# A 25th place for expert weights, requests without a limit, and the last norm's rows by transposes

## The reference

```python
e_idx, gate = route(xf, w_router, b_router)      # best group of 4, its top 2 of 32
y = moe_ffn(xf, e_idx, gate, w_gate, w_up, w_down)
#   per expert: h = silu(xb @ w_gate[e]) * (xb @ w_up[e]);  h @ w_down[e]
x = layer_norm(DEEPNORM_ALPHA * x + y, ln_g[2], ln_b[2])
```

## Time and profile before

| | us |
|---|---|
| three runs | 1108.01, 1110.08, 1111.56; median 1110.08 |
| the profiled execution | 1108.52 |
| its span | 1106.8 |
| PE busy | 1033.0 (93%) |
| DVE, ACT, POOL busy | 343.2, 251.5, 101.6 |

### The profile page before, as it was taken

One profiled execution on the slowest core, in us unless ns is written; L12 is line 12 of the kernel. 1 busy time (PEld: TensorE's weight loads), 2 busy tenths in 40 slices (PEclk: granted clock), 3 DMA queues, 4 the chain that ended last, 5 costly groups with the idle time before them and its releaser, 6 DMA issues.

```text
span 1106.8 us, 15722 instructions
## 1 busy us (share of the span) xinstructions
PE 1033.0 (93%) x6596; PEld 516.4 (47%) x6596; DVE 343.2 (31%) x724; ACT 251.5 (23%) x510; POOL 101.6 (9%) x141
## 2 busy tenths in 40 slices
PE   8999999999898999999999999999999999887896
PEld 4444455557655554566544733333333333333342
DVE  0179623234655645203215511111111111011015
ACT  2341122234435520013401111111111111011023
POOL 2000100000000000100000211111111111110123
PEclk9999999999999999999999999999999999999999
DMA  8012320211222150553833899999999999999995
GB/s 274 23 65 76 115 77 2 78 43 51 63 77 80 76 191 1 181 236 113 311 121 121 341 417 419 423 419 418 419 416 422 415 423 414 416 417 408 417 415 210
DMA packets 57462, 265.73 MB, mean 240 GB/s; under 512 B 7122, under 2 KB 8274, under 8 KB 32560
## 3 DMA queue, kind: packets, MB, share of 16 engines
q1 hardware_dynamic: 51200, 255.49, 58.2%
q0 software_dynamic: 4960, 8.15, 2.0%
q10 hardware_dynamic: 1232, 1.08, 0.3%
HBM read 256.56 MB, written 16.25 MB: 246 GB/s over the span
## 4 chain that ended last, share of the span: by engine, by line
PE 34%; DMA 20%; DVE 3%; ACT 1%; issue 1%; DVEq 0%; SPq 0%; ACTq 0%
PE cpair L2051 7%; DMA ring<-in_w_exp_up 7%; PE bank L2061 6%; DMA xT<-in_w_exp_up 4%; DMA ring<-in_w_exp_down 4%; PE tpair L2051 4%; DMA keys<-in_w_exp_up 3%; DMA ar<-in_w_exp_down 3%; PE bank L1890 2%; PE bank L1870 2%; PE tpair L1890 1%; PE bank L1863 1%; PE cpair L1890 1%; PE tpair L1870 1%; PE cpair L1870 1%; PE bank L2033 1%
## 5 line engine op out<-in xcount | busy, mean ns | idle before, releaser
L2051 PE MATMUL cpair<-ring,xgT 128*64 128x512 f32 x344 | 115.0, 598 | 6.4 <-DMA xT<-in_w_exp_up 4.1
L2491 DVE TENSOR_TENSOR hs<-cpair,hs 64x512 f32<-64x512 f32 x21 | 14.5, 693 | 252.4 <-ACT hs L2273 252.4
L2273 ACT ACTIVATE hs<-cpair 64x512 f32<-64x512 f32 x21 | 12.4, 588 | 235.5 <-PE cpair L2051 235.5
L2051 PEld LDWEIGHTS cpair<-ring,xgT 128*64 128x64 f32 x344 | 36.0, 138 | 58.4 <-issue 58.4
L1793 POOL DMA_INDIRECT y_rows<-ye,tabs x30 | 30.5, 1018 | 352.2 <-ACT xgt L2279 331.3
L922 PE MATMUL bank<-xT,ring 128*128 128x512 f32 x128 | 60.9, 606 | 0.0
L2051 PE MATMUL tpair<-ring,xgT 128*64 128x512 f32 x168 | 56.5, 593 | 0.0
L365 PE MATMUL bank<-xT,ring 128*128 128x512 f32 x112 | 48.5, 593 | 0.0
L2491 DVE TENSOR_TENSOR hs<-tpair,hs 64x512 f32<-64x512 f32 x11 | 7.6, 693 | 125.5 <-ACT hs L2273 125.5
L941 PE MATMUL tpair<-ring,mixT 128*128 128x512 f32 x96 | 42.0, 594 | 0.0
L2061 PE MATMUL bank<-ring,hT 128*64 128x512 f32 x128 | 32.4, 653 | 4.1 <-DVE hT L2495 4.1
(11 more groups left out here) (479 smaller groups left out, 1913.5 us busy)
## 6 DMA issues: line engine op xcount, KB each, us to landing
ring<-in_w_exp_up SPq DMA_DIRECT2D x32, 1024.0 KB, 10.2
ring<-in_w_exp_gate SPq DMA_DIRECT2D x32, 1024.0 KB, 10.4
ring<-in_w_exp_down SPq DMA_DIRECT2D x16, 1024.0 KB, 10.6
ring<-in_w_in SPq DMA_DIRECT2D x6, 2048.0 KB, 8.1
ring<-in_w_mem_kv SPq DMA_DIRECT2D x4, 2048.0 KB, 10.3
opening<-in_w_exp_gate SPq DMA_DIRECT2D x8, 1024.0 KB, 10.3
mixT<-in_w_exp_down SPq DMA_DIRECT2D x8, 1024.0 KB, 10.5
mixT<-in_w_exp_gate SPq DMA_DIRECT2D x8, 1024.0 KB, 10.4
```

What stands on the lines that cost most here:

```text
L2051: last = nc.tensor.matmul(bank[b][m * CAP:(m + 1) * CAP, :], xgT[:, j, h, :], w(m, h)[:, j * DE:(j + 1) * DE], start=(k == 0), stop=(k == ...
L2491: V.tensor_tensor(hb, bank[1 + e % 3][CAP:P, :], sil, ALU.mult).then_inc(h_done, 1)
```

## The change

- `lists_at` is now the 25th place, and `extra` is two tiles. SP asks pieces 21, 22 and 23 right behind piece 20 (22 after `lg_full`, 23 after `lt_full`), piece 24 at `tabs_done`; it waits for neither `asked` nor `comb_done`. From piece 25 on a request waits only for its place.
- The space: `xgt` shrinks to `xg`, the gathered rows alone. Half of `x2T` gets a tile of its own for the routing (`x2_high`), `first_rows` writes into `ye` and DVE adds in place, `combT` and `comb` move to freed places. `first_rows(e)` now waits for the scatter of expert e - 2 out of the same buffer; DVE does `out_rows(e - 1)` before `hidden(e)`.
- `comb` is built in expert 28 from the comparisons made anew (`last_hit`), and turned in expert 29. Before, DVE built it between the routing's tables.
- `ln3`: in expert 28 PE transposes a broadcast column of `cols` for each of the 16 blocks of 128, and ACT copies the banks. POOL's `spread`, `ones3` and PE's L2135 go.
- At the end `down(31)` comes before `combined(0, 0)`.

```diff
-        NPL = len(places) + 2
+        NPL = len(places) + 3
...
-        extra = sb("extra", [P, HALF])
-        places += [extra[:, :], lists_at[:, :]]
+        extra = [sb(f"extra{i}", [P, HALF]) for i in range(2)]
+        places += [extra[0][:, :], extra[1][:, :], lists_at[:, :]]
...
                     load_piece(sp, 20)
+                    load_piece(sp, 21)
+                    sp.wait_ge(lg_full, 2)
+                    load_piece(sp, 22)
+                    sp.wait_ge(lt_full, 2)
+                    load_piece(sp, 23)
 
                 def experts():
-                    sp.wait_ge(asked, 1)
-                    load_piece(sp, NPL - 3)
                     sp.wait_ge(tabs_done, 1)
-                    load_piece(sp, NPL - 2)
-                    sp.wait_ge(comb_done, 1)
                     load_piece(sp, NPL - 1)
                     for n in range(NPL, len(stream)):
                         e, i, h = stream[n - NPL]
                         sp.wait_ge(w_read, read_at[e, DN if i == 2 else GU, h])
-                        piece_here(sp, n - 4)
                         load_piece(sp, n)
...
-                        if e == LAST - 2:
-                            down_read(pool, e)
-                            pool.memset(ones3, 1.0).then_inc(spread_done, 1)
-                            for h, name in enumerate(("n3_g", "n3_b")):
-                                at = ROWS[name][0]
-                                pool.tensor_tensor(spread[:, h, :, :], ident[:, :].unsqueeze(1).to_broadcast([P, KT, P]),
-                                                   cols[:, at:at + KT].unsqueeze(2).to_broadcast([P, KT, P]), ALU.mult)\
-                                    .then_inc(spread_done, 1)
...
-                        if e == 0:
+                        if e == LAST - 2:
                             tables_turned()
...
+                    def last_norm(h):
+                        pe.wait_ge(ln3_here, 2 * h)
+                        at = ROWS[("n3_g", "n3_b")[h]][0]
+                        for hf in range(2):
+                            for j in range(4):
+                                c = at + 4 * hf + j
+                                last = nc.tensor.transpose(bank[6 + hf][:, j * P:(j + 1) * P],
+                                                           cols[:, c:c + 1].to_broadcast([P, P]), ident[:, :])
+                            last.then_inc(ln3_full, 1)
 
                     tokens(0)
                     for e in range(NE):
-                        if e == LAST:
-                            last_norm()
                         products_of(e)
+                        if e == LAST - 3:
+                            last_norm(0)
...
+                    down(f)
                     pe.wait_ge(y_scaled, LAST)
-                    pe.wait_ge(ln3_here, 4)
+                    pe.wait_ge(comb_read, 2)
                     combined(0, 0, True)
-                    down(f)
                     combined(1, 0, True)
...
                         if e >= 2:
-                            act.wait_ge(y_scaled, e - 1)
-                        nc.scalar.activation(xrow[:, e % 2, :], xg[:, e % 2, :], ACT.Copy,
+                            act.wait_ge(y_out[e % 2], 16 * (e // 2))
+                        nc.scalar.activation(ye[:, e % 2, :], xg[:, e % 2, :], ACT.Copy,
                                              scale=tabs[:, e, 3:4].bitcast(F32)).then_inc(x_done, 1)
...
+                    def combination():
+                        gu_read(dve, LAST - 3)
+                        for k in range(TOP_K):
+                            rows = slice(k * NT, (k + 1) * NT)
+                            V.tensor_tensor(last_hit[:, rows, :], ls.caps[:, :].unsqueeze(1).to_broadcast([P, NT, 2 * CAP]),
+                                            ls.place[:, rows].unsqueeze(2).to_broadcast([P, NT, 2 * CAP]), ALU.is_equal)\
+                                .then_inc(last_hits, 1)
...
                     for e in range(NE):
+                        if 0 < e < LAST:
+                            out_rows(e - 1)
                         hidden(e)
-                        if e:
+                        if e == LAST:
                             out_rows(e - 1)
...
                         turned(e)
+                        if e == LAST - 3:
+                            combination()
```

More of the change, by code:

```diff
@@ L1406, in hybrid_decoder_trunk @@
         xg_here = [sem(f"xg_here{s}") for s in range(2)]
-        xgt = sb("xgt", [P, 2, D])
-        xg, xrow = (xgt[:, i, :].rearrange("p (b c) -> p b c", b=2) for i in range(2))
+        xg = sb("xg", [P, 2, D // 2])
         def slots_of(dve, ls):
@@ L1593, in hybrid_decoder_trunk @@
             <= read_at[LAST - 2, DN, 1]
-        yb = [free[t].rearrange("p (k d) -> p k d", k=TOP_K) for t in range(NT)]
-        hs2 = free[4][:, 0:DE]
-        hb2, sil2 = hs2[0:CAP, :], hs2[CAP:P, :]
[L1597 to L1607, removed]
+        ln3 = free[0].rearrange("p (h d) -> p h d", h=2)
+        last_hit = free[1][:, 0:D].rearrange("p (r c) -> p r c", c=2 * CAP)
+        comb = free[1][:, D:2 * D].rearrange("p (a t c) -> p a t c", a=2, t=NT)
+        combT = free[2][:, 0:2 * S].rearrange("p (a s) -> p a s", a=2)
+        yb = [free[3 + t].rearrange("p (k d) -> p k d", k=TOP_K) for t in range(NT)]
+        ob = [free[(7, 10)[t // 2]][:, (t % 2) * D:(t % 2 + 1) * D] for t in range(NT)]
+        spare = free[11].rearrange("p (b d) -> p b d", b=2)
+        x3 = [yb[t][:, 0, :] for t in range(NT)]
+        further_piece = lambda i, h: free[(5, 6, 7, 10, 11, 12)[2 * i + h]]
+        hs2, yf, xf = (free[8][:, i * 512:(i + 1) * 512] for i in range(3))
+        hb2, sil2 = hs2[0:CAP, :], hs2[CAP:P, :]
+        tabs2 = free[8][:, 1536:1536 + 4 * NE].bitcast(I32).rearrange("p (e f) -> p e f", f=4)
+        ls2 = Lists(kept, free[9])
+        ln3_full, ln3_here, last_hits = sem("ln3_full"), sem("ln3_here"), sem("last_hits")
         acc = ((6, 7), (3, 1), (2, 4), (5, 0))
@@ L1840, in body @@
                             pool.wait_ge(f_ys, g)
-                            scatter(rowc[:, :], ye[:, 0, :]).then_inc(f_out, 16)
+                            scatter(rowc[:, :], yf).then_inc(f_out, 16)
                             pool.wait_ge(f_out, g * 16)
@@ L2125, in body @@
                             down_terms(5, hT[:, 0, :, :], further_piece, 1).then_inc(f_y, 1)
[L2127 to L2135, removed]
-                                                 spread[:, h, 4 * hf:4 * hf + 4, :].rearrange("p j q -> p (j q)"),
-                                                 start=True, stop=True).then_inc(ln3_full, 1)
+                    def last_norm(h):
[7 more added lines that the diff above has]
+                            last.then_inc(ln3_full, 1)
                     tokens(0)
                     for e in range(NE):
-                        if e == LAST:
-                            last_norm()
                         products_of(e)
+                        if e == LAST - 3:
+                            last_norm(0)
                         if e == LAST - 1:
@@ L2315, in experts @@
                             first_rows(e + 1)
+                        if e == LAST - 3:
+                            last_norm(1)
                     act.wait_ge(set_done, 1)
@@ L2470, in routing @@
                     link(dve, V.tensor_copy(more_i[:, :], ls.most_f[:, :]))
-                    def combination(a):
-                        for t in range(NT):
-                            link(dve, V.tensor_scalar(comb[:, a, t, :], ls.hit[:, t, :], last_oh[:, 0, t, a:a + 1], None,
-                                                      ALU.mult))
-                            last = V.scalar_tensor_tensor(comb[:, a, t, :], ls.hit[:, NT + t, :],
-                                                          last_oh[:, 1, t, a:a + 1], comb[:, a, t, :], ALU.mult, ALU.add)
-                        return last
                     link(dve, V.tensor_copy(last_oh[:, :, :, :], oh[:, 0:TOP_K, :, LAST - 1:NE]))
@@ L2499, in out_rows @@
                         dve.wait_ge(x_done, e + 1)
-                        if e >= 2:
-                            dve.wait_ge(y_out[e % 2], 16 * (e // 2))
-                        if e == 0:
-                            dve.wait_ge(comb_full, 1)
                         down_read(dve, e)
-                        V.scalar_tensor_tensor(ye[:, e % 2, :], bank[5 if e < LAST else 0][:, :], tabs[:, e, 2:3].bitcast(F32), xrow[:, e % 2, :],
+                        V.scalar_tensor_tensor(ye[:, e % 2, :], bank[5 if e < LAST else 0][:, :], tabs[:, e, 2:3].bitcast(F32), ye[:, e % 2, :],
                                                ALU.mult, ALU.add).then_inc(y_scaled, 1)
+                    def combination():
[5 more added lines that the diff above has]
+                                .then_inc(last_hits, 1)
+                        dve.wait_ge(last_hits, TOP_K)
+                        for a in range(2):
```

(6 more changed lines are left out.)

44 lines of the change are left out of this document (20 added, 24 removed).

## The result

The changed kernel takes 1114.87 us (median of 6 runs, 1112.83 to 1117.4), the kernel before 1109.59 beside it (6 runs, 1107.83 to 1111.56): ratio 1.0050, 95% interval 1.0036 to 1.0063. It is slower by 5.3 us, beyond what the prediction called measurable and above its range.

A forecast was written before the change was run, and what follows sets the result against it. The DMA engines' fixed amount to move after 617 us was taken to bound the kernel, PE's floor 11.4 us away. Terms -0.55 + 0 + 0 + 0.3 = -0.25 us gained, added to 1110.08, gave 1110.3; range 1104.5 to 1113.5.

The forecast's parts named there:

- What bounds the kernel: From 640 us the DMA engines are never idle; their fixed amount sets the end, PE's own floor 11.4 us away.
- D: How much later PE starts expert 0's tokens because the first gather lands behind queued pieces: 3.8 us.
- the 25th place's worth is nearly all given back: At the first reuse of a place: of 2.5 us, a gain of 4.1 - 3.8 = 0.3 us stays.
- the sum: All parts of the change over the whole kernel: -0.55 + 0 + 0 + 0.3 = -0.25 us gained.
- a low clock at 632 costs 1.7 us before the first place is read: PE after its 3.6 us wait for the first gather: 1.7 us lost, even chance, middle -0.55 with the gather's part.
- POOL's third add is tied to the reads: At the end PE arrives 2.2 us earlier, but the add follows the y_rows landings: 0.3 us gained.
- No limit of four, 0 us: SP's piece requests in steady state: engines already busy 1.01, no idle time to win, taken as 0.
- rival 2: The DMA rate rises with the deep queue by 1% or more: 4.4 us on top, 1105.9; chance 0.16.
- Scatter order, moved tables: Scatter landings of 6.3 to 7.0 us stay hidden under 18 us; moved work at experts 28 and 29 costs 0.
- 1 (lead kept): First gather lands in time, D near 0: gain 4.0 us, 1106.1; chance 0.10.
- 3 (small transfers wait for the depth): Every expert's small transfers wait for the queue's depth, holding first_rows on ACT: 195 us, about 1305; chance 0.04.
- 4: First gather served strictly after the pieces asked before it: D = 5.8, gain -3.1 us, 1113.2; chance 0.08.

The follow-up runs named there:

- r4_dummies: Changed kernel with 31 more pairs of dummy transposes on PE before expert 0's tokens (UNREAD[3] 34 instead of 3); 1115.86 us, ratio 1.0049.
- r9_cover: Changed kernel with 15 more pairs of dummy transposes before expert 0's token transposes, to fill PE's wait for the first gather; 1111.08 us, ratio 1.0012.
- r7_both: r1_asked with piece 21 asked right behind piece 20 and PE's last products for all tables ahead of those with POOL's rows; 1106.25 us, ratio 0.9969.
- r1_asked: Changed kernel with SP again waiting for the first gather to be asked before piece 21; 1110.57 us, ratio 1.0006.
- r3_both: Changed kernel with both the wait for the first gather's request before piece 21 and the limit of four back; 1111.04 us, ratio 1.0001.
- r10_after_again: Changed kernel without any edit, measured again in a second session; 1114.46 us, ratio 1.0033.
- r2_limit: Changed kernel with the limit of four back (SP waits for piece n - 4 before asking for n); 1113.48 us, ratio 1.0028.
- r8_before_nolimit: Kernel before the change with only the limit of four taken out; 1110.55 us, ratio 1.0005.
- r12_before_early21: Kernel before the change, with 24 places, and piece 21 asked right behind piece 20; 1111.37 us, ratio 1.0007.
- r5_tail: r1_asked with PE's last products for all tables ahead of all products with POOL's rows; 1108.96 us, ratio 0.9990.
- r11_both_limit: r7_both with the limit of four requests put back; 1107.61 us, ratio 0.9978.

## Why the prediction was wrong

It forecast 1110.3 and no measurable change; the kernel is slower by 5.3 us. By its own steps:

- **What bounds the kernel.** Held. The DMA share is 1.01 from 645 on in both. Counted from the request of piece 20, and less the engines' idle time from 623 to 645 (1.0 to 7.2 us), POOL's first add comes at 461.9 to 463.9 us in all fourteen profiles. So it follows the idle time within 2 us; the latest of them, r4_dummies and the two with both edits, are 1.9 us behind the changed kernel, and why is open.
- **D and "the 25th place's worth is nearly all given back".** Held: D was forecast 3.8 us; the tokens were turned at 633.53 against 628.22 + 1.57 for the shift, 3.74. r9_cover, where nothing else of the loss before 645 is left, is idle 3.7 us as before; the sum gave 0.3 us less.
- **"By the rows a low clock at 632 costs 1.7 us before the first place is read; I give it an even chance."** This is the first step that failed, in size and in its chance; that a low clock would cost time was right. It was there in all three profiles with the wait of 3.6 us left uncovered, it cost 2.8 us (9.90, 9.94 and 9.98 us for 32 products, 7.11 with the wait covered), and the engines' idle time grew by 3.1 us, where the sum had a loss of 0.55. The 1.7 came from the only rows at hand: 5.35 us against 3.65 for sixteen products. It is not a fixed price: sixteen products took 6.42 us in the changed kernel at 1072.44. Neither the number of products nor the wait just ahead sorts these sizes: 2.97 us came before a loss of 1.7 in rows 9, 3.59 before 2.8 here, 1.31 before 2.8 at 1070, and 0.52 before 1.7 in r7_both at 640. What sets them stays open; the mistake was to take one case as the price. The granted clock in the window at 634, right after the wait, is 0.53, a mean over the two levels. The Trainium skill's rule (TensorE: Matmul & The Clock Gate, "What's actually happening"), that the low clock is the default and activity releases it, agrees with that window.
- **"POOL's third add is tied to the reads. PE can only take what stood between 1091.14 and 1091.78; I count 0.3 us of it."** The second step that failed, in sign. PE does arrive early, and gains nothing by it. The third add is not tied to the reads alone: with VectorE's norm beside it it takes 3.1 us where the sum had 2.36, so the slack it counted was not there. Of the eight profiles with the tail as the change leaves it six show PE waiting 3.0 to 3.2 us for the third add, and four of these (r1_asked, r3_both, r9_cover, r10_after_again) run on at low clock: from the first pair of products with POOL's rows to the third 6.7 to 6.8 us, against 3.8 in the two others and in the kernel before. That is 3.0 us for those executions. In the other two, the changed kernel's first profile and r2_limit, a low clock in expert 31's products makes PE late instead, and the tail is 24.8 and 24.9 us. Over the eight its mean is 25.2 us; it is 22.8 to 22.9 in the kernel before, r8_before_nolimit and r12_before_early21. r5_tail, which splits the wait, has a tail of 22.7 us and gains 1.8 us over r1_asked by the ratios.
- **No limit of four, 0 us.** Held in the time: r8_before_nolimit stands at 1.0005, and r2_limit and r3_both are not told apart from the same kernels without the limit. Not in the trace: the mean rate from 645 to 1076 rose to 421 GB/s from 418, 0.7%, which would be 3.1 us, two thirds of rival 2. It was given back at the end, where the queue drains unevenly (below): in r7_both and r11_both_limit POOL's first add, less the shift by piece 20's request, comes at 1082.0 and 1082.1, without and with the limit.
- **Scatter order, moved tables.** Held: the scatters land in 6.6 us, ACT's 2.0 us of waiting for them in three experts reach nobody, and PE waits nowhere for the moved work.
- **The rivals.** 1 (lead kept) fell; 3 (small transfers wait for the depth) fell clearly, with a request landing 27 us after it was made while scatters took 6.6, and 6.8 with four at most in the queue. The Trainium skill's rule that engines take turns between queues (DMA: Bandwidth & Descriptors, "Queues, rings and completion order") agrees with these scatters. 4 named the right direction and nearly the size for the wrong reason: D was 3.74, not 5.8.

The sum with the measured terms is 4.1 - 3.74 - 2.8 = -2.4 us for the DMA engines, and 22.9 - 25.2 = -2.3 for the tail, together -4.7; measured -5.3 and, the second time, -4.3 by the medians. How often an execution has the low clock in the tail is known only from these few profiles, so that term is the softest. For a single profile the split above is firm; for the median it is an estimate.

## What to carry to other kernels

Before filling a gap in a busy queue, look at what small transfer was quick because of the gap, and let as many requests pass ahead of it as the engines can finish before it comes: one here, not three. A wait of some 3 us on PE is priced with the slow products that may follow it: 1.7 to 3 us in most of these traces, nothing in some. Work taken off PE ahead of such a wait only lengthens it, so the work left should be laid into the wait or between two. Where places and order depend on each other, test both alone and together: each alone left the engines idle for 3.4 us, the two together for 1.1, and that is some 2 us of r7_both's 3.4; the rest is the tail's.

## What the runs showed of the hardware that was not expected

- *A low clock need not cost time.* In r7_both sixteen down products of expert 0 took 5.35 us instead of 3.65 at 640.18 (granted clock 0.66 over 640 to 645), with no wait over 0.75 us among expert 0's products, and it is the fastest kernel. PE waits 11 us for pieces after that, so the 1.7 us are likely taken out of those waits; no run takes the slow products alone away.
- *Without the limit the transfers fade out instead of stopping.* The windows of the changed kernel, and then of r2_limit, which asks for piece 20 only 0.2 us earlier and has the limit, show it in the DMA share of the same two stretches. Over the next 4 us it is 0.13 and 0.17, over the 8 us ahead 0.98 and 1.01. That the 16 engines get ahead of one another in a deep queue would explain it; no run measured an engine by itself.

```profile
1084.00:1088.00 4.00, 3.48 (x19) 1.50 (x15) 1.17 (x2) 0.44 (x2) 0.50 (x1) 1.00 0.78 317
1088.00:1092.00 4.00, 4.00 (x20) 1.41 (x18) 0.75 (x1) 0.00 (x0) 3.82 (x2) 1.00 0.46 186
```

```profile
1084.00:1088.00 4.00, 3.48 (x19) 1.58 (x17) 1.18 (x2) 0.68 (x2) 0.00 (x0) 1.00 1.02 411
1088.00:1092.00 4.00, 4.00 (x22) 1.29 (x20) 0.75 (x1) 0.00 (x0) 3.78 (x2) 1.00 0.88 354
```

- *POOL and VectorE slow each other at the end.* POOL's adds of 128x1024 take 2.35 us alone and 3.1 to 3.3 (6.42 for two in r7_both) beside VectorE's norm. A VectorE pass that takes 1.28 us behind POOL's last add took 3.13 in the changed kernel beside it, while that add kept its 2.35.
- *A shift that has nothing to do with the change.* From 457 us of the span on, 32 products took 12.06 us in the changed kernel's profile and 10.59 before; the time of piece 20's request, 616.6 to 620.4 over all profiles, varies from one profile to the next, with and without the change (617.2, 618.7 and 619.9 in the three kernels with 24 places). A span is compared from an event behind such a place, or 1.6 us are given a wrong cause.
